# Multiplying exponentials by their inverse sums on ScalarE in place of VectorE, in four attention bodies of an encoder step

## The chip, the cores and the metric

One core of a Trainium2 chip. The time is the device time of one execution in microseconds, the median of a few runs. Before the change it is 1914.42 us (three runs, 1914.21 to 1914.43).

## The reference

One layer of a streaming encoder, run for 256 prompt frames and 32 new frames that share the weights (together 288 columns). In order: half a SwiGLU feed-forward block, a mixer with three groups of attention heads (A: sparse with an indexer, B: sliding window with sinks, C: chunk band), and another half feed-forward block. Cut to what matters here:

```python
def swiglu_ffn(x, g, w_gate, w_up, w_down):
    h = rmsnorm(x, g)
    return (jax.nn.silu(h @ w_gate) * (h @ w_up)) @ w_down

def attend(q, k, v, bias, mask, sinks):
    s = jnp.einsum('btkgd,blkd->bkgtl', qg, k).astype(jnp.float32) * ATTN_SCALE + bias
    p = jax.nn.softmax(s, axis=-1)                  # C
    m = jnp.maximum(jnp.max(s, axis=-1, keepdims=True), sk)      # B, with sinks
    e = jnp.exp(s - m)
    p = e / (jnp.sum(e, axis=-1, keepdims=True) + jnp.exp(sk - m))
    return jnp.einsum('bkgtl,blkd->btkgd', p, v)

x = x + 0.5 * swiglu_ffn(x, *ffn1)
z = rmsnorm(x, g) @ w_in                            # queries, keys, values of all heads
x = x + concat(A, B, C) @ w_out
x = x + 0.5 * swiglu_ffn(x, *ffn2)
```

## The kernel before

Activations lie transposed, 128 features on the partitions and the 288 frames along the row. Every weight matrix is read in strips of 128 output features, 16 tiles of 128x128 at most. Full precision comes from splitting: ScalarE copies the strip `raw` to `w_hi` in a shorter type (line 1117, two halves of 1024 columns), VectorE subtracts to get `w_lo` (line 1444, two halves), and TensorE (PE) does three products for each tile: `w_hi` with the upper and the lower part of the activations (lines 643, 644) and `w_lo` with the upper part (line 645). A strip of 16 tiles is 48 matmuls and takes about 6 us. PE waits for the first half of `w_lo` (`lo_rdy`) before the first tile, for the second before the ninth. SyncE loads strips into two buffers.

The mixer's input projection runs in phases. In phase "cb" (20 strips), the first four strips are projected alone; then come four bodies, each projecting four strips while it does the attention of the pair of heads of groups C and B that the four strips before made. The changed lines count these bodies 0 to 3 and call the attention of the last C and B pair and of group A, which runs in phase "a" and beside "wo", the bodies from 4 on.

A body has five units: 0 and 1 for pair 0 (group C), 2 and 3 for pair 1 (group B), 4 for the 32 new frames of both. Units 0 and 2 hold the later 128 frames, which see 256 keys; units 1 and 3 the earlier 128 frames with 128 keys. A unit holds two heads, so its scores `s_buf` are two rows of 256 or 128 columns for each frame. PE's order in a body is written out (`attention`, line 793): piece 0 (a strip), scores of units 0 to 3, a transpose of values, piece 1, transposes of the probabilities of units 0 and 1 (`tp`, line 749), piece 2, scores of unit 4, outputs of pair 0, transposes of units 2 and 3, piece 3, transposes of unit 4, sums of squares, the other outputs.

ScalarE and VectorE follow in four steps, also in written order (`attention_pairs`, lines 1233 and 1579). In step 0 VectorE adds scale and bias to the scores of units 0 and 1 and takes their maxima (`smax`), and reads a product; ScalarE does their exponentials with sums (`exps`, line 1173); VectorE adds the sink where there is one, takes the inverses of the sums (line 1560) and multiplies the exponentials by them (`inverse`, line 1564); then both split the strip of piece 2. Step 1 does the same for units 2 and 3 and the strip of piece 3, step 2 for unit 4 and piece 0 of the next body, step 3 the key norms and piece 1 of the next body. The engines meet by semaphores alone: `mx_rdy` (maxima), `e_rdy` (exponentials), `r_rdy` (inverses), `p_rdy` (probabilities; PE waits for it in `turn_p`, line 752), `hi_rdy` and `lo_rdy` (splits).

Of the kernel before, what the change touches and what calls it, by code (L numbers as in the profile page):

```python
# [8 lines left out]
ACT = mybir.ActivationFunctionType  # L9
# [104 lines left out]
def encoder_step(nc, x, cak, cav, caki, cbk, cbv, cck, ccv, w_in, w_out, qk_norm, sinks, c_bias, t5_bias,  # L114
# [17 lines left out]
    with ctx:  # L132
        def sb(name, shape, dt=F32, scope=ctx):
            return scope.enter_context(nc.sbuf_tensor(name, shape, dt))

        def sem(name):
            return ctx.enter_context(nc.semaphore(name))
# [87 lines left out]
        s_buf = [sb(f"s_buf{s}", [P, 2, T_P]) for s in range(2)]  # L225
# [13 lines left out]
        einv = [sb(f"einv{s}", [P, 2]) for s in range(2)]  # L239
# [69 lines left out]
        e_rdy = sem("exponentials_ready")  # L309
        r_rdy = sem("inverse_sums_ready")  # L310
        p_rdy = sem("probabilities_ready")
        t_done = sem("probabilities_transposed")
        c_done = sem("transposed_copied")
        pv_done = sem("unit_output_done")
# [43 lines left out]
        NKEY = [T_P, P, PAST + T_S]  # L358
        UNITS = 5
        PAIR_OF, ROWS_OF = (0, 0, 1, 1, None), (0, 1, 0, 1, 2)  # L360
# [8 lines left out]
        def at_once(body):  # L369

            return not (isinstance(body, int) and body >= 4)
# [9 lines left out]
        def v_turn_bank(m):  # L381

            return bank_m if isinstance(m, int) and m == MISC_A0 else bank_t[1]
# [8 lines left out]
        def buf(ph, s):  # L392
            return (ph.n0 + s) % 2
# [103 lines left out]
        RUN0 = 4 * UNITS  # L497
# [26 lines left out]
        def s_slot(U, u):  # L524

            return (U + u) % 4 if isinstance(U, int) and U >= RUN0 else (0, 1, 0, 1, 2)[u]
# [107 lines left out]
        def _(pe):  # L634
# [114 lines left out]
            def turn_p(U, u, slot):  # L749

                b, r = u % 2, ROWS_OF[u]
                pe.wait_ge(p_rdy, U + (u + 1))
                if not (isinstance(U, int) and U + u < 2):
                    pe.wait_ge(c_done, U + (0, 0, 1, 2, 3)[u])
                if r == 2:
                    pe.transpose(bank_t[b][:, 0:P], s_buf[slot][:, 0, 0:P], ident[:, :])
                    mm = pe.transpose(bank_t[b][0:T_S, P:2 * P], s_buf[slot][:, 0, P:P + T_S], ident[:, :])
                else:
                    for c in range(2):
                        for kc in range(NKEY[r] // P):  # L760
                            o = (c * (NKEY[r] // P) + kc) * P
                            mm = pe.transpose(bank_t[b][:, o:o + P], s_buf[slot][:, c, kc * P:(kc + 1) * P], ident[:, :])  # L762
                mm.then_inc(t_done, 1)
# [320 lines left out]
        def _(act):  # L1084
# [61 lines left out]
            def set_deviation(m, b, keys, pairs):  # L1146

                act.wait_ge(m_done, m + 1)

                if keys:  # L1150
                    if not (isinstance(b, int) and b == 0):
                        act.wait_ge(kinv_rdy, b)
                    else:
                        act.wait_ge(rinv_rdy, KEY_NORMS)
                else:
                    act.wait_ge(scale_rdy, scale_no("a", b, pairs[0]) - 1)
                    if isinstance(b, int):
                        act.wait_ge(kinv_rdy, 5)
                c0, c1 = (NT + c for c in scale_cols(pairs))
                act.activation(sd[:, 0 if keys else c0:c1], misc_bank(m)[:, 0 if keys else c0:c1], ACT.Sqrt, bias=eps[:, :]).then_inc(m_free, 1)  # L1160

            def place_v(m, v, cols, bank=None):
                act.wait_ge(m_done, m + 1)
                bank = bank or misc_bank(m)
                act.activation(v[:, 0:2, cols], bank[:, 0:2 * P].rearrange("p (t c) -> p t c", t=2), ACT.Copy)
                act.activation(v[0:T_S, 3, cols], bank[0:T_S, 2 * P:3 * P], ACT.Copy).then_inc(m_free, 1)

            def exps(U, u, sink, sign=1.0):
                b, r = u % 2, ROWS_OF[u]
                n, slot = NKEY[r], s_slot(U, u)  # L1170
                act.wait_ge(mx_rdy, U + (u + 1))
                for c in range(1 if r == 2 else 2):
                    a = act.activation(s_buf[slot][:, c, 0:n], s_buf[slot][:, c, 0:n], ACT.Exp, bias=nmax[b][:, c:c + 1], scale=sign,  # L1173
                                       accum_out=esum[b][:, c:c + 1])
                if sink and r == 2:
                    a = act.activation(esnk[b][HD:P, 0:1], snk[b][HD:P, 0:1], ACT.Exp)
                elif sink:
                    a = act.activation(esnk[b][:, :], snk[b][:, :], ACT.Exp)
                a.then_inc(e_rdy, 1)

            def copy_t(U, u):
                b, r = u % 2, ROWS_OF[u]
                act.wait_ge(t_done, U + (u + 1))
                before = (-1, -1, 2, 2, 0)[u]
                if not (isinstance(U, int) and U + before < 1):

                    act.wait_ge(pv_done, U + before)
                pt = bank_t[b][:, :].rearrange("p (t c) -> p t c", t=4)
                if r == 0:
                    a = act.activation(p_pair[:, :, 1:3, :], pt.rearrange("p (h k) c -> p h k c", h=2), ACT.Copy)  # L1190
                elif r == 1:
                    a = act.activation(p_pair[:, :, 0, :], pt[:, 0:2, :], ACT.Copy)
                else:
                    act.activation(p_t[r][:, 0:1, :], pt[:, 0:1, :], ACT.Copy)
                    a = act.activation(p_t[r][0:T_S, 1:2, :], pt[0:T_S, 1:2, :], ACT.Copy)
                a.then_inc(c_done, 1)

            def out_hi(U, p, tiles):
                act.wait_ge(pv_done, U + (UNITS if p else 2))
                if p == 0:  # L1200
                    a = act.activation(o_hi[:, tiles[0], :, 0:T_P // 2], two_rows(bank_o[:, 0:T_P]), ACT.Copy)
                else:
                    act.activation(o_hi[:, tiles[1], :, :], two_rows(bank_o[:, 0:NT]), ACT.Copy)
                    a = act.activation(o_hi[:, tiles[0], :, T_P // 2:NT // 2], two_rows(bank_o[:, S_OUT[0]]), ACT.Copy)
                a.then_inc(ohi_rdy, 1)
# [27 lines left out]
            def attention_pairs(body, turn, splits, tiles, sums):  # L1233

                U = body * UNITS
                for j in range(4):
                    if j == 0:
                        act.wait_ge(v_out, body * 32 + VOUT_PREP * 32)
                        if not (isinstance(body, int) and body == 0):
                            act.wait_ge(pv_done, U)  # L1240
                        place_v(turn, v_c, slice(0, P), v_turn_bank(turn))
                    elif j < 3:
                        copy_t(U, 2 * j - 2)
                        copy_t(U, 2 * j - 1)
                    else:
                        copy_t(U, 4)
                    if j < 2:
                        exps(U, 2 * j, j == 1)
                        exps(U, 2 * j + 1, j == 1)
                    elif j == 2:  # L1250
                        exps(U, 4, True)
                        out_hi(U, 0, tiles)
                    else:
                        set_deviation(*sums)
                    split(splits[j])
                out_hi(U, 1, tiles)
# [163 lines left out]
        def _(dve):  # L1420
# [130 lines left out]
            def inverse(kind, body, u):  # L1551
                b, r, p = u % 2, ROWS_OF[u], PAIR_OF[u]
                slot = s_slot(body * UNITS, u)
                heads = slice(0, 1 if r == 2 else 2)
                dve.wait_ge(e_rdy, body * UNITS + (u + 1))
                if kind == "cb" and p != 0:
                    rows = slice(HD, P) if r == 2 else slice(0, P)
                    dve.tensor_tensor(esum[b][rows, heads], esum[b][rows, heads], esnk[b][rows, heads], ALU.add).then_inc(sum_sunk, 1)
                    dve.wait_ge(sum_sunk, body * 3 + (r + 1))
                dve.reciprocal(einv[b][:, heads], esum[b][:, heads]).then_inc(r_rdy, 1)  # L1560
                dve.wait_ge(r_rdy, body * UNITS + (u + 1))
                n = NKEY[r]
                for c in range(1 if r == 2 else 2):
                    ins = dve.tensor_scalar(s_buf[slot][:, c, 0:n], s_buf[slot][:, c, 0:n], einv[b][:, c:c + 1], None, ALU.mult)
                ins.then_inc(p_rdy, 1)
# [185 lines left out]
            for ph in phases:  # L1751
# [97 lines left out]
                elif ph.name == "prep":  # L1849
# [12 lines left out]
                    b = buf(ph, 0)  # L1862
# [333 lines left out]
```

## Time and profile before

| | |
|---|---|
| median of three runs | 1914.42 us |
| profiled execution | 1913.98 us |
| its span, first to last instruction | 1912.4 us |
| PE busy | 1905.0 us (100%) |
| VectorE (DVE) busy | 1150.7 us (60%) |
| ScalarE (ACT) busy | 835.6 us (44%) |
| DMA, mean over the span | 178 GB/s |

All times in the rows are microseconds from the start of the span unless marked as ns. A row of a timeline has the start, the length, the engine, the line of the kernel, the operation, what it writes and reads, and how many follow each other; in brackets the idle time before it and what ended that. A row's length is that of the whole run of instructions from the first start to the last end; instructions on one engine overlap a little, so the next may start before the end of the one before. PEld is the loading of weights into PE, which runs beside its matmuls. Shares of the whole span say little here: feed-forward and attention have different limits, so the four bodies (868 to 992 us) are looked at apart.

### The profile page before, as it was taken

To read this page: it belongs to the slowest core of one execution; us is meant where nothing else is said; L and a number is where in the kernel's file an instruction comes from. 1 tells how busy PE (TensorE), PEld (TensorE's weight loads), DVE (VectorE), ACT (ScalarE), POOL (GpSimd) and SP (SyncE) were. 2 spreads that over 40 slices of the span, in tenths; PEclk is the share of its full clock that TensorE was granted. 3 is DMA by queue.
4 is the path that set the end of the run, shared out by engine and by line. 5 is a ranking of instruction groups with operands and counts; after the bars stand their busy time and mean duration, and the time that the engine had idled before them with its cause. 6 is when DMAs were issued, how large, how long until landed. Compare 5 with 4: busy or idle time off the path is not lost.

```text
span 1912.4 us, 41753 instructions
## 1 busy us (share of the span) xinstructions
PE 1905.0 (100%) x15725; PEld 1885.5 (99%) x15725; DVE 1150.7 (60%) x1714; ACT 835.6 (44%) x1223; POOL 131.1 (7%) x237
## 2 busy tenths in 40 slices
PE   9999999999999999999999999999999999999999
PEld 8999999999999999999998999999999999999999
DVE  7555445555555566588888765555545555455554
ACT  6443333343333344445668644333334443333332
POOL 1000000000000000124665000000000000000000
DMA  7555555555555555655554555555555555555564
GB/s 270 180 180 172 185 171 178 179 183 176 184 176 175 175 176 176 194 167 167 164 183 123 165 180 177 182 177 174 181 174 181 179 178 175 184 175 178 180 196 154
DMA packets 102298, 340.62 MB, mean 178 GB/s; under 512 B 12661, under 2 KB 17317, under 8 KB 102224
## 3 DMA queue, kind: packets, MB, share of 16 engines
q1 hardware_dynamic: 95856, 329.41, 52.9%
q0 software_dynamic: 3984, 8.11, 1.7%
q10 hardware_dynamic: 2400, 2.33, 0.3%
q8 instruction: 36, 0.59, 0.1%
q14 instruction: 22, 0.18, 0.0%
HBM read 335.10 MB, written 5.28 MB: 178 GB/s over the span
## 4 chain that ended last, share of the span: by engine, by line
PE 97%; DVE 1%; ACT 1%; issue 0%; DMA 0%; POOL 0%; SPq 0%; POOLq 0%; DVEq 0%; ACTq 0%
PE bank L643 32%; PE bank L645 31%; PE bank L644 31%; PE bank L745 1%; PE bank L762 0%; PE bank L777 0%; DMA raw<-in_w_ffn_gate 0%; PE bank L711 0%; PE bank L963 0%; PE bank L789 0%; DVE h_hi_and_lo L1713 0%; ACT s_buf L1173 0%; PE bank L780 0%; DVE w_lo L1444 0%; DVE w_lo L1721 0%
## 5 line engine op out<-in xcount | busy, mean ns | idle before, releaser
L643 PE MATMUL bank<-h_hi_and_lo,w_hi 128*128 128x288 f32 x3344 | 961.2, 287 | 1.8 <-DVE w_lo L1721 1.6
L644 PE MATMUL bank<-h_hi_and_lo,w_hi 128*128 128x288 f32 x3344 | 956.5, 286 | 0.0
L645 PE MATMUL bank<-h_hi_and_lo,w_lo 128*128 128x288 f32 x3344 | 956.4, 286 | 0.0
L1444 DVE TENSOR_TENSOR w_lo<-raw,w_hi 128x1024 fp32r<-128x1024 f32 x634 | 727.9, 1189 | 205.4 <-ACT w_hi L1117 205.1
L1117 ACT ACTIVATE w_hi<-raw 128x1024 fp32r<-128x1024 f32 x634 | 616.7, 1020 | 289.5 <-PE bank L645 272.6
L643 PEld LDWEIGHTS bank<-h_hi_and_lo,w_hi 128*128 128x128 f32 x3344 | 632.0, 189 | 6.8 <-issue 3.0
L644 PEld LDWEIGHTS bank<-h_hi_and_lo,w_hi 128*128 128x128 f32 x3344 | 632.2, 189 | 0.2
L645 PEld LDWEIGHTS bank<-h_hi_and_lo,w_lo 128*128 128x128 f32 x3344 | 632.1, 189 | 0.0
L643 PE MATMUL bank<-gu_hi_and_lo,w_hi 128*128 128x288 f32 x1376 | 393.5, 286 | 0.0
L644 PE MATMUL bank<-gu_hi_and_lo,w_hi 128*128 128x288 f32 x1376 | 393.5, 286 | 0.0
L645 PE MATMUL bank<-gu_hi_and_lo,w_lo 128*128 128x288 f32 x1376 | 393.5, 286 | 0.0
L643 PEld LDWEIGHTS bank<-gu_hi_and_lo,w_hi 128*128 128x128 f32 x1376 | 260.1, 189 | 0.0
L644 PEld LDWEIGHTS bank<-gu_hi_and_lo,w_hi 128*128 128x128 f32 x1376 | 260.1, 189 | 0.0
L645 PEld LDWEIGHTS bank<-gu_hi_and_lo,w_lo 128*128 128x128 f32 x1376 | 260.1, 189 | 0.0
L1350 ACT ACTIVATE gu_hi_and_lo<-gu 128x288 f32 (+1 forms) x86 | 40.6, 472 | 348.8 <-DVE gu L1790 348.8
L1346 ACT ACTIVATE g_sig<-g_act 128x288 f32<-128x288 f32 x86 | 38.1, 442 | 240.6 <-DVE g_act L1468 240.6
L1832 DVE SCALAR_TENSOR_TENSOR gains_and_x<-bank,gains_and_x 128x288 f32 (+1 forms) x96 | 43.9, 457 | 155.7 <-PE bank L645 154.8
L1468 DVE TENSOR_TENSOR u_act<-bank,rstd 128x288 f32<-128x288 f32 x86 | 39.3, 457 | 122.6 <-PE bank L645 122.6
L1468 DVE TENSOR_TENSOR g_act<-bank,rstd 128x288 f32<-128x288 f32 x86 | 39.3, 458 | 76.4 <-PE bank L645 76.3
L1795 DVE TENSOR_TENSOR gu_hi_and_lo<-gu,gu_hi_and_lo 128x288 f32 (+1 forms) x86 | 39.5, 459 | 70.0 <-ACT gu_hi_and_lo L1350 69.9
L643 PE MATMUL bank<-o_hi_and_lo,w_hi 128*128 128x288 f32 x256 | 73.9, 289 | 0.0
L644 PE MATMUL bank<-o_hi_and_lo,w_hi 128*128 128x288 f32 x256 | 73.2, 286 | 0.0
(227 smaller groups left out, 964.6 us busy)
## 6 DMA issues: line engine op xcount, KB each, us to landing
raw<-in_w_ffn_gate SPq DMA_DIRECT2D x168, 512.0 KB, 4.5
raw<-in_w_ffn_up SPq DMA_DIRECT2D x168, 512.0 KB, 4.6
raw<-in_w_ffn_down SPq DMA_DIRECT2D x96, 512.0 KB, 3.8
raw<-in_w_in SPq DMA_DIRECT2D x74, 512.0 KB, 4.7
raw<-in_w_ffn_down SPq DMA_DIRECT2D x64, 384.0 KB, 4.2
raw<-in_w_out SPq DMA_DIRECT2D x32, 512.0 KB, 4.5
raw<-in_w_ffn_down SPq DMA_DIRECT2D x32, 448.0 KB, 4.3
bias_rev<-bias_vectors POOLq DMA_DIRECT2D x11, 256.0 KB, 5.9
```

The source lines that it names most:

```text
L643: pe.matmul(out, w_hi[b][:, k, :], hi, start=(k == first_k), stop=False)
L644: pe.matmul(out, w_hi[b][:, k, :], lo, start=False, stop=False)
L645: mm = pe.matmul(out, w_lo[b][:, k, :], hi, start=False, stop=(k == last_k))
L745: mm = pe.matmul(score_place(body, u, c), q[p][half, FULL[r]], kt[p][half, KEY0[r]:KEY0[r] + NKEY[r]], start=True, stop=True)
L1117: act.activation(w_hi[b][:, k, :], raw_tile(ph, j, s)[:, k, :], ACT.Copy).then_inc(hi_rdy, 1)
L1346: act.activation(g_sig[:, :], g_act[:, :], ACT.Silu).then_inc(sig_rdy, 1)
L1350: act.activation(gu_hi[:, j, :, :], two_rows(gu[:, :]), ACT.Copy).then_inc(guh_rdy, 1)
L1444: dve.tensor_tensor(w_lo[b][:, k, :], raw_tile(ph, j, s)[:, k, :], w_hi[b][:, k, :].bitcast(F32), ALU.subtract)\
L1468: return dve.tensor_tensor(dst, (early_bank(n) or bank_w[b])[rows, cols], rstd[rows, cols], ALU.mult)
L1795: dve.tensor_tensor(gu_lo[:, j, :, :], two_rows(gu[:, :]), gu_hi[:, j, :, :].bitcast(F32), ALU.subtract).then_inc(gul_rdy, 1)
L1832: dve.scalar_tensor_tensor(dst, src[:, 0:NT], factor, xT[:, d, :], ALU.mult, ALU.add)\
```

## The change

In bodies 0 to 3 the multiplies of units 0 and 2 (256 keys, two heads each) are taken out of VectorE's `inverse`, which returns behind the inverse. ScalarE gets a function `weigh`: it waits for the inverse and does the two multiplies as `Copy` with the inverse as scale of each partition. It is called in steps 0 and 1 behind both units' exponentials and ahead of the split. A new semaphore `p_act` tells PE that units 0 and 2 are done; the counts of `p_rdy` are renumbered. Units 1, 3 and 4 and all bodies from 4 on stay as they were.

```diff
@@ turn_p (PE)
-                pe.wait_ge(p_rdy, U + (u + 1))
+                if U < RUN0 and r == 0:
+                    pe.wait_ge(p_act, U // UNITS * 2 + (PAIR_OF[u] + 1))
+                elif U < RUN0:
+                    pe.wait_ge(p_rdy, U // UNITS * 3 + (u // 2 + 1))
+                else:
+                    pe.wait_ge(p_rdy, RUN0 // UNITS * 3 + U - RUN0 + (u + 1))
@@ ScalarE
+            def weigh(U, u):
+
+                b, slot = u % 2, s_slot(U, u)
+                act.wait_ge(r_rdy, U + (u + 1))
+                for c in range(2):
+                    a = act.activation(s_buf[slot][:, c, 0:NKEY[0]], s_buf[slot][:, c, 0:NKEY[0]], ACT.Copy, scale=einv[b][:, c:c + 1])
+                a.then_inc(p_act, 1)
...
                     if j < 2:
                         exps(U, 2 * j, j == 1)
                         exps(U, 2 * j + 1, j == 1)
+                        weigh(U, 2 * j)
@@ inverse (VectorE)
                 n = NKEY[r]
+                if r == 0 and at_once(body):
+                    return
```

ScalarE before, steps 0 and 1 of body 0 (`p_pair` holds transposed probabilities, `esnk` the exponentials of the sinks):

```order
L1173 ACTIVATE s_buf,esum<-s_buf,nmax 128x256 x2
L1173 ACTIVATE s_buf,esum<-s_buf,nmax 128x128 x2
L1117 ACTIVATE w_hi<-raw 128x1024 x2
L1190 ACTIVATE p_pair<-bank 128x2x256
L1192 ACTIVATE p_pair<-bank 128x2x128
L1173 ACTIVATE s_buf,esum<-s_buf,nmax 128x256 x2
L1178 ACTIVATE esnk<-snk 128x2
L1173 ACTIVATE s_buf,esum<-s_buf,nmax 128x128 x2
L1178 ACTIVATE esnk<-snk 128x2
L1117 ACTIVATE w_hi<-raw 128x1024 x2
```

The same place of the changed kernel (its line numbers are a little higher):

```order
L1179 ACTIVATE s_buf,esum<-s_buf,nmax 128x256 x2
L1179 ACTIVATE s_buf,esum<-s_buf,nmax 128x128 x2
L1192 ACTIVATE s_buf<-s_buf,einv 128x256 x2
L1123 ACTIVATE w_hi<-raw 128x1024 x2
L1204 ACTIVATE p_pair<-bank 128x2x256
L1206 ACTIVATE p_pair<-bank 128x2x128
L1179 ACTIVATE s_buf,esum<-s_buf,nmax 128x256 x2
L1184 ACTIVATE esnk<-snk 128x2
L1179 ACTIVATE s_buf,esum<-s_buf,nmax 128x128 x2
L1184 ACTIVATE esnk<-snk 128x2
L1192 ACTIVATE s_buf<-s_buf,einv 128x256 x2
L1123 ACTIVATE w_hi<-raw 128x1024 x2
```

Two pairs of activations are new, each directly ahead of a split (`w_hi`); nothing else moved on this engine.

VectorE before, the end of step 1 of body 0 (`esum` the sums, `einv` their inverses, `z_q` a product that is read):

```order
L1468 TENSOR_TENSOR z_q<-bank,rstd 128x288
L1558 TENSOR_TENSOR esum<-esum,esnk 128x2
L1560 RECIPROCAL einv<-esum 128x2
L1564 TENSOR_SCALAR s_buf<-s_buf,einv 128x256 x2
L1558 TENSOR_TENSOR esum<-esum,esnk 128x2
L1560 RECIPROCAL einv<-esum 128x2
L1564 TENSOR_SCALAR s_buf<-s_buf,einv 128x128 x2
L1444 TENSOR_TENSOR w_lo<-raw,w_hi 128x1024 x2
```

And in the changed kernel:

```order
L1483 TENSOR_TENSOR z_q<-bank,rstd 128x288
L1573 TENSOR_TENSOR esum<-esum,esnk 128x2
L1575 RECIPROCAL einv<-esum 128x2
L1573 TENSOR_TENSOR esum<-esum,esnk 128x2
L1575 RECIPROCAL einv<-esum 128x2
L1581 TENSOR_SCALAR s_buf<-s_buf,einv 128x128 x2
L1459 TENSOR_TENSOR w_lo<-raw,w_hi 128x1024 x2
```

The two multiplies of 256 columns are gone, and the rest keeps its order.

## Rows read from the trace of the kernel before

**Rows 1.** The page: span, and the engines' shares of the last chain.

```profile
span 1912.4 us, 41753 instructions
...
PE 97%; DVE 1%; ACT 1%; issue 0%; DMA 0%; POOL 0%; SPq 0%; POOLq 0%; DVEq 0%; ACTq 0%
```

**Rows 2.** Stretches, bodies 0, 3: length, busy PE, PEld, DVE, ACT, POOL, clock, DMA.

```profile
868.40:899.00 30.60, 30.60 (x284) 29.40 (x284) 26.29 (x61) 18.91 (x42) 14.18 (x21) 1.00 0.54 168
...
960.40:991.60 31.20, 30.97 (x284) 29.41 (x284) 27.84 (x66) 18.96 (x44) 18.05 (x31) 1.00 0.54 167
```

**Rows 3.** PE's waits in the four bodies: us in total, times, longest.

```profile
PE bank L643 <- DVE w_lo L1444: 0.2, 1, 0.2
```

**Rows 4.** Timeline of PE: transposes, then the next piece's first matmul (bodies 0, 3).

```profile
882.17 0.82 PE L762 MATMUL bank<-ident,s_buf 128*128 128x128 f32 x6
882.75 0.37 PE L643 MATMUL bank<-h_hi_and_lo,w_hi 128*128 128x288 f32 x1
...
889.88 0.87 PE L762 MATMUL bank<-ident,s_buf 128*128 128x128 f32 x6
890.57 0.36 PE L643 MATMUL bank<-h_hi_and_lo,w_hi 128*128 128x288 f32 x1
...
974.16 0.82 PE L762 MATMUL bank<-ident,s_buf 128*128 128x128 f32 x6
975.21 0.36 PE L643 MATMUL bank<-h_hi_and_lo,w_hi 128*128 128x288 f32 x1 [0.23 <-DVE w_lo L1444]
```

**Rows 5.** Timeline of ACT: the splits for pieces 2 and 3.

```profile
880.07 0.19 ACT L1173 ACTIVATION_READ_ACCUMULATOR s_buf<-s_buf,nmax 128x1 f32 x1
880.17 1.99 ACT L1117 ACTIVATE w_hi<-raw 128x1024 fp32r<-128x1024 f32 x2
...
887.79 1.99 ACT L1117 ACTIVATE w_hi<-raw 128x1024 fp32r<-128x1024 f32 x2
...
941.25 1.99 ACT L1117 ACTIVATE w_hi<-raw 128x1024 fp32r<-128x1024 f32 x2
...
972.46 1.99 ACT L1117 ACTIVATE w_hi<-raw 128x1024 fp32r<-128x1024 f32 x2
```

**Rows 6.** Timeline of DVE: low parts for pieces 2 and 3, and around them.

```profile
881.24 2.36 DVE L1444 TENSOR_TENSOR w_lo<-raw,w_hi 128x1024 fp32r<-128x1024 f32 x2
883.52 0.87 DVE L1526 SCALAR_TENSOR_TENSOR s_buf<-bank,q_scale,bias_rev 128x256 f32<-128x256 f32 x2
...
887.35 0.17 DVE L1560 RECIPROCAL einv<-esum 128x2 f32<-128x2 f32 x1
887.55 0.91 DVE L1564 TENSOR_SCALAR s_buf<-s_buf,einv 128x256 f32<-128x256 f32 x2
...
889.21 1.22 DVE L1444 TENSOR_TENSOR w_lo<-raw,w_hi 128x1024 fp32r<-128x1024 f32 x1
...
942.62 2.35 DVE L1444 TENSOR_TENSOR w_lo<-raw,w_hi 128x1024 fp32r<-128x1024 f32 x2
...
973.53 1.53 DVE L1444 TENSOR_TENSOR w_lo<-raw,w_hi 128x1024 fp32r<-128x1024 f32 x1 [0.24 <-ACT w_hi L1117]
...
976.12 0.86 DVE L1526 SCALAR_TENSOR_TENSOR s_buf<-bank,q_scale,bias_rev 128x256 f32<-128x256 f32 x2
```

**Rows 7.** Groups in the four bodies: count | busy us, mean ns | idle before.

```profile
L1564 DVE TENSOR_SCALAR s_buf<-s_buf,einv 128x256 f32<-128x256 f32 x16 | 6.3, 437 | 0.3
```

**Rows 8.** ACT, timeline rows and groups: what is nearest to the added copies.

```profile
878.40 0.51 ACT L1173 ACTIVATE s_buf<-s_buf,nmax 128x256 f32<-128x256 f32 x1
878.81 0.19 ACT L1173 ACTIVATION_READ_ACCUMULATOR s_buf<-s_buf,nmax 128x1 f32 x1
...
10.90 1.45 ACT L1127 ACTIVATE h_hi_and_lo<-gains_and_x 128x288 fp32r<-128x288 f32 x3
...
L1127 ACT ACTIVATE h_hi_and_lo<-gains_and_x 128x288 fp32r<-128x288 f32 x26 | 13.6, 552 | 1.7 <-DMA gains_and_x<-in_gains_and_x 1.7
...
L1299 ACT ACTIVATE w_hi<-raw 128x256 fp32r<-128x256 f32 x2 | 0.8, 410 | 0.1
```

More of the change, by code:

```diff
@@ L311, in encoder_step @@
         p_rdy = sem("probabilities_ready")
+        p_act = sem("probabilities_ready_by_scalar")
         t_done = sem("probabilities_transposed")
```

## The prediction

> **What bounds the kernel now.** I read the page's busy times and chain first. The chain that ended last is 97% PE over a span of 1912.4 us [rows 1], so a VectorE or ScalarE instruction costs time only where PE is made to wait. The second view is the table of stretches, one per attention body: the first of the four bodies that the diff touches lasts 30.6 us and the last 31.2, with PE busy for all of it but 0.2 us in the last, and the granted clock at 1.00 (its upper level) [rows 2]. VectorE is busy 26 to 28 us of each, ScalarE 19 us: neither is full, both have places where they are late.
>
> The list of PE's waits names one such wait, for a low half of a weight strip (`w_lo`), 0.2 us [rows 3]. The timeline shows more than that list. Between pieces of projection PE does six 128x128 transposes and then the first matmul of the next piece. Where nothing is late this matmul starts 0.58 us after the transposes (882.17 to 882.75); ahead of piece 3 of body 0 it takes 0.69 (889.88 to 890.57), and ahead of piece 2 of body 3 1.05 (974.16 to 975.21) [rows 4]. The VectorE row that makes the first half of that strip's `w_lo` started at 889.21 and took 1.22; 889.21 + 1.36 = 890.57 [rows 4, 6]. The same 1.36 or 1.37 us from start of `w_lo` to start of the piece holds at five places of these bodies: piece 3 of all four and piece 2 of body 2. So there PE already starts when the first half of the strip's low part is there; on the three other pieces 2 the slack is 0.15 and 0.21 us (bodies 0 and 1) and none (body 3, where the half took 1.53 us instead of 1.22 [rows 6]). All these small stalls together (start distances above 0.58) come to about 1.2 us. Whatever delays the first half of `w_lo` in front of pieces 2 and 3 delays PE, nearly one for one.
>
> **What the change does to that chain.** In front of pieces 2 and 3 each engine goes through the same order: ScalarE does the exponentials and then the two halves of `w_hi`; VectorE does sums, inverses, multiplies and then the two halves of `w_lo`, each of which waits for its half of `w_hi`. Where VectorE waits, `w_lo` starts 1.07 us after `w_hi` (972.46 to 973.53) [rows 5, 6]; I take 1.08.
>
> Removed from VectorE: two multiplies of 256 columns at each of two places in four bodies, 16 in all, 437 ns each by the mean, 6.3 us busy [rows 7]. The pair in front of piece 3 of body 0 takes 0.91 us [rows 6].
>
> Added to ScalarE: the same 16 as copies with a per-partition scale, placed before the two `w_hi` halves, so `w_hi` moves back by the pitch of two. No such row exists at 256 columns. The nearest: the exponential of 256 columns with a per-partition bias lasts 0.51, and the next instruction starts 0.41 us after it [rows 8]. A copy with a per-partition scale at 288 columns lasts 0.552, three take 1.45, a pitch of (1.45 - 0.55)/2 = 0.45 us; it also reads and writes with a stride [rows 8]. A plain copy of 256 columns lasts 0.410; less the overlap of 0.10 seen at the exponential, 0.31 [rows 8]. So between 0.31 and 0.45; I take 0.40, nearest to the row with the same number of columns and a pointer operand. A pair is A = 0.80 us, with ends 0.62 and 0.90. No table load is added: `w_hi`, a copy too, follows the exponentials with no load between them (880.07, 880.17) [rows 5].
>
> The added wait: the copies wait for VectorE's inverse. In front of piece 3 of body 0 that ends at 887.35 + 0.17 = 887.52, and ScalarE is free for it at 887.79 [rows 5, 6]; 0.27 us to spare. In front of piece 2 there is as much or more. Behind the waiting copy stand `w_hi` and, behind that, the copies of the transposes; PE wants the probabilities (transposes at 882.17 and 889.88) a microsecond after the copies end, so the new semaphore itself costs nothing.
>
> Step by step, with the margin = start of `w_lo` now, minus start of `w_hi`, minus 1.08 (what VectorE was late by itself):
> - Piece 2, body 0: 881.24 - 880.17 - 1.08 = about 0, so `w_lo` starts 0.81 later. Body 1 repeats it within 0.01 us: 0.80.
> - Piece 2, body 2: 942.62 - 941.25 - 1.08 = 0.29, so 0.51 later.
> - Piece 2, body 3: starts 0.81 later, but the first half then takes 1.22 and not 1.53. Two halves pass in 2.28 us (881.24 to 883.52), so VectorE is free at 972.46 + 0.80 + 1.08 + 2.28 = 976.62 in place of 976.12: 0.50 later [rows 5, 6].
> - From there VectorE's next units, the exponentials and the split for piece 3 all start later by the same amount, since ScalarE waits there for VectorE's maxima. PE's delay at piece 2 is so carried into the next term and isn't counted twice.
> - Piece 3: margin 889.21 - 887.79 - 1.08 = 0.34 [rows 5, 6], and 0.34 or 0.35 in all four bodies. It adds A - 0.34 = 0.46 to each.
>
> Delay of PE at piece 3: body 0 0.81 + 0.46 = 1.27; body 1 1.26; body 2 0.51 + 0.45 = 0.96; body 3 0.50 + 0.46 = 0.96. Sum 4.45 us; in A it is 8A - 1.95. Behind piece 3 nothing is given back: the later splits of a body and the next body's first steps follow PE's own products, and have two microseconds and more to spare. The loads wait for `w_lo` of the strip before, so they move with it. In the other phases no line changes.
>
> The profiled execution took 1913.98, the runs' median is 1914.42, 0.44 more; both get 4.45: 1918.43 and **1918.87**. I forecast 1918.9 us. What can be told from no change is 0.2%, or 3.83 us; my sum is above it by 0.6, and falls below it if a pair costs less than 0.72 us. By the ends of A the sum is 3.0 and 5.25.
>
> The Trainium skill speaks of this choice. "Perfetto Trace Analysis", section "Optimizing Scalar/DVE Operations", puts ScalarE's overhead on SBUF at about 93 ns of engine time. By an estimate from that page (93 ns and 256 columns at 1.2 GHz) a copy would take 0.31 us, the pair 0.61, and the sum would be 2.9 us. The exponential's row, with its 0.41, speaks against it, so I hold that the pointer operand is paid too.
>
> **Rivals.**
> - Cheap copies: a pitch of 0.31 to 0.35 as in the plain copy [rows 8]. Sum 3.0 to 3.7, 1917.4 to 1918.1 us: slower, but not by 0.2%. Against it: the pitch of both rows with a pointer. Chance 0.16.
> - Not slower: the multiplies leave VectorE, the busier of the two, and its lateness at piece 3 (0.34) and at piece 2 of body 2 (0.29) is what holds PE up there. If ScalarE took the copies in time that it waits (it stands idle for VectorE's maxima and PE's transposes), only the gain would stay: at most the stalls of 1.2 us, 1913.2, and 1914.4 if nothing waits either way. It decides in favour where a pair delays `w_hi` by less than 1.95/8 = 0.24 us. Against it: in the order the copies stand directly before the split, behind exponentials that end late. The skill's same section says that work may go to ScalarE where DVE is saturated, which would bring this out; the stretches (26 to 28 of 31 us busy) show it near that but not there. Chance 0.10.
> - Dear copies: the pitch of 0.45, or a wait for the inverse that ends late by over 0.27 us because VectorE shares its time with POOL there. Sum 5.3 to 6.5, 1919.7 to 1920.9. Against it: the spare 0.27. Chance 0.14.
>
> **How the numbers follow.** My forecast (3.7 to 5.2, 1918.1 to 1919.6) has 0.60. Slower by over 0.2%: 0.55 of that and 0.14 of dear copies, 0.69. Within 0.2%: the rest of mine (0.05), cheap copies (0.16), and most of not slower (0.07), 0.28. Faster by over 0.2% would need 3.8 us where PE stalls 1.2 in all: 0.03. The range 1917.0 to 1920.3 takes in both ends of A and leaves out not slower and the far end of dear copies.
>
> **What the changed profile would show.** Copies of 0.49 us with a pitch of 0.40 before `w_hi`, 16 of them, and 6.3 us less on VectorE; VectorE now waiting for `w_hi` at all eight places, some 1.2 to 1.7 us each (what it loses there plus the multiplies that it no longer does); PE waiting for `w_lo` ahead of pieces 2 and 3 in every body; bodies about 1.0 to 1.3 us longer, the first 31.9 and the last 32.2 us; nothing else longer. It would be wrong if the copies stand in ScalarE's idle time, if a body after its piece 3 gets time back, or if PE waits for the transposed probabilities and not for `w_lo`.

## The result and the profile after

The changed kernel takes 1918.52 us (median of 11 runs, 1917.84 to 1919.48), the kernel before 1913.79 (11 runs, 1912.79 to 1914.71): a ratio of 1.0026, 95% interval 1.0019 to 1.0034, or 4.7 us slower. The profiled execution took 1919.29 us over a span of 1917.7, 5.3 more than before [rows 1]. One execution in the experiments, of the kernel with a bias load held back, took 2474.20 us, where its ten others took 1917.67 to 1918.99.

The added copies first: a summary of their line, and ScalarE's timeline in front of pieces 2 and 3 of body 0 (start, length, engine, line).

```profile
L1192 ACT ACTIVATE s_buf<-s_buf,einv x16: 492/494/497, 880.3 to 984.6; 128x256 f32<-128x256 f32 x16
```

```profile
880.35 0.89 ACT L1192 ACTIVATE s_buf<-s_buf,einv 128x256 f32<-128x256 f32 x2
881.15 1.99 ACT L1123 ACTIVATE w_hi<-raw 128x1024 fp32r<-128x1024 f32 x2
...
888.77 0.89 ACT L1192 ACTIVATE s_buf<-s_buf,einv 128x256 f32<-128x256 f32 x2
889.57 1.99 ACT L1123 ACTIVATE w_hi<-raw 128x1024 fp32r<-128x1024 f32 x2
```

Sixteen copies of 494 ns, and `w_hi` follows a pair 0.80 us after its start: a pitch of 0.40. In [rows 5] `w_hi` started at 880.17 and 887.79.

VectorE's timeline at the same places, then what VectorE and what PE waited for in the four bodies (total us, times, longest):

```profile
882.22 2.36 DVE L1459 TENSOR_TENSOR w_lo<-raw,w_hi 128x1024 fp32r<-128x1024 f32 x2 [0.88 <-ACT w_hi L1123]
...
890.64 2.36 DVE L1459 TENSOR_TENSOR w_lo<-raw,w_hi 128x1024 fp32r<-128x1024 f32 x2 [0.80 <-ACT w_hi L1123]
```

```profile
DVE w_lo L1459 <- ACT w_hi L1123: 6.5, 8, 0.9
```

```profile
PE bank L644 <- DVE w_lo L1459: 3.3, 8, 0.4
```

The rows of the 256-key multiplies [rows 7] are gone: 6.3 us less work on VectorE, and 6.5 us of waiting for `w_hi` there, where before only one wait stood, of 0.24 [rows 6]. VectorE now waits for as long as it was relieved. PE, which waited once for `w_lo` [rows 3], waits at all eight places.

PE's timeline shows it at body 0:

```profile
882.36 0.82 PE L768 MATMUL bank<-ident,s_buf 128*128 128x128 f32 x6
883.59 0.36 PE L644 MATMUL bank<-h_hi_and_lo,w_hi 128*128 128x288 f32 x1 [0.42 <-DVE w_lo L1459]
...
890.71 0.88 PE L768 MATMUL bank<-ident,s_buf 128*128 128x128 f32 x6
892.01 0.36 PE L644 MATMUL bank<-h_hi_and_lo,w_hi 128*128 128x288 f32 x1 [0.42 <-DVE w_lo L1459]
```

From the transposes to the next piece 1.23 and 1.30 us, in [rows 4] 0.58 and 0.69. And 882.22 + 1.37 = 883.59, 890.64 + 1.37 = 892.01: the piece still starts 1.37 us after its `w_lo`.

The first matmul of each piece can be followed like this through all kernels. The table says how much later it comes than in the first execution of before, with the lateness that the execution already had at the start of body 0 subtracted (those starts scatter from -0.59 to +1.10 us between executions, where the code is the same in all). Columns: pieces 2 and 3 of bodies 0 to 3; the third and fourth piece after body 3 (pieces there are thirds of a pair of strips); a late piece, at 1069. "1st", "2nd" and "3rd" are profiled executions of the same kernel; the later ones belong to the experiments below. All later tables are of this kind.

| | b0 p2 | b0 p3 | b1 p2 | b1 p3 | b2 p2 | b2 p3 | b3 p2 | b3 p3 | 1002.6 | 1009.5 | 1069 |
|---|---|---|---|---|---|---|---|---|---|---|---|
| predicted | 0.81 | 1.27 | 2.07 | 2.53 | 3.04 | 3.49 | 3.99 | 4.45 | 4.45 | 4.45 | 4.45 |
| changed, 1st profile | 0.66 | 1.26 | 1.86 | 2.51 | 3.01 | 3.47 | 3.68 | 4.14 | 4.51 | 5.19 | 5.16 |
| changed, 2nd | 0.67 | 1.28 | 1.90 | 2.57 | 3.08 | 3.55 | 3.76 | 4.23 | 4.55 | 5.24 | 5.24 |
| changed, 3rd | 0.66 | 1.26 | 1.86 | 2.52 | 3.02 | 3.48 | 3.68 | 4.15 | 4.71 | 5.38 | 5.33 |
| before, 2nd | -0.01 | 0.00 | -0.01 | 0.00 | -0.10 | -0.29 | -0.31 | -0.31 | -0.32 | -0.31 | -0.35 |

Two things come out. The bodies cost 4.14 to 4.23 us, stepwise nearly as forecast. Then, behind piece 3 of body 3, where no line was changed, PE loses another 1.0 to 1.2 us. From the last column on nothing is added: in the first profile PE is 5.34 us later at 1069 (5.16 and the 0.18 of the start of body 0), and the span is 5.3 longer.

### The profile page after: what moved, and what is told of

Read it like the earlier page. It is cut to its first block, busy times and chain, and to the rows that moved or that the text cites. A ratio compares the mean times of both kernels' runs of the same rounds, so it can differ in the third digit from the quotient of the medians.

```text
span 1917.7 us, 41761 instructions
## 1 busy us (share of the span) xinstructions
PE 1906.1 (99%) x15725; PEld 1885.3 (98%) x15725; DVE 1143.9 (60%) x1698; ACT 842.0 (44%) x1239; POOL 122.4 (6%) x237
## 4 chain that ended last, share of the span: by engine, by line
PE 94%; DVE 2%; ACT 2%; issue 1%; DMA 0%; POOL 0%; SPq 0%; POOLq 0%; DVEq 0%; ACTq 0%
PE bank L644 31%; PE bank L646 31%; PE bank L645 31%; DVE w_lo L1459 1%; ACT s_buf L1179 0%; PE bank L746 0%; DVE s_buf L1541 0%; ACT w_hi L1123 0%; DMA raw<-in_w_ffn_gate 0%; DVE nmax L1553 0%; PE bank L768 0%; PE bank L969 0%; ACT s_buf L1192 0%; PE bank L712 0%; PE bank L783 0%
```

## The experiments

The theory: ScalarE's copies stand in the chain exponentials, `w_hi`, `w_lo`, PE, and each pair delays it by 0.80 us; VectorE's relief is worth nothing. The rivals: the loss belongs to one of the two steps; it comes from the new semaphore or the renumbered counts; VectorE's relief gives something back that hides a larger cost. A second question is the loss behind body 3.

### One step at a time

The copies of unit 0 only, or of unit 2 only; the other stays with VectorE. The edits of this section are shown against the changed kernel, shortened, with `...` for what is left out.

```diff
-                        weigh(U, 2 * j)
+                        if j == 0:        # second kernel: j == 1
+                            weigh(U, 2 * j)
...
-                if r == 0 and at_once(body):
+                if u == 0 and at_once(body):        # second kernel: u == 2
```

> The copies of step 0 alone (units 0) on ScalarE; units 2 are multiplied on VectorE as before. Theory (a pair of copies ahead of the split delays the low half of the strip by what it lasts, 0.80 us, less what VectorE was late by itself): 0.8, 0.8, 0.5 and 0.2 to 0.5 us in bodies 0 to 3, 2.3 to 2.6 in all, about 1916.2 us, and in front of piece 3 nothing is added to it. Rival (PE waits for probabilities from ScalarE): no wait for w_lo ahead of piece 3 but one ahead of the transposes. Rival (the relief of VectorE counts): half of the changed kernel's loss or less.

> The copies of step 1 alone (units 2) on ScalarE; units 0 are multiplied on VectorE as before. Theory: nothing ahead of piece 2, 0.46 us ahead of piece 3 in each body, 1.84 in all; with step 0 alone the two add up to the changed kernel's 4.1 to 4.5 in the bodies. Behind body 3 the changed kernel lost about 1 us more, where ScalarE waited 1.5 us for a strip's load; if that comes from VectorE standing idle ahead of piece 3 it shows here too: 1915.6 us without, 1916.7 with it.

Step 0 alone: 1916.38 us (ratio 1.0015, 1.0006 to 1.0024). Step 1 alone: 1916.50 (1.0015, 1.0006 to 1.0024); the kernel before, beside them, 1913.67.

| | b0 p2 | b0 p3 | b1 p2 | b1 p3 | b2 p2 | b2 p3 | b3 p2 | b3 p3 | 1002.6 | 1009.5 | 1069 |
|---|---|---|---|---|---|---|---|---|---|---|---|
| step 0 | 0.65 | 0.79 | 1.39 | 1.59 | 2.09 | 2.10 | 2.30 | 2.30 | 2.29 | 2.30 | 2.32 |
| step 1 | 0.00 | 0.47 | 0.46 | 0.93 | 0.82 | 1.08 | 0.63 | 1.71 | 2.42 | 3.10 | 3.10 |

Step 0 delays pieces 2, step 1 pieces 3, and the parts come near the whole: 2.30 + 1.71 = 4.01 against 4.14 to 4.23 for both. The loss is two terms of one kind, not one bad place. That the sum comes so near is in part luck: step 1's 1.71 isn't four times 0.46. Its pieces 3 pay 0.47, 0.47, 0.26 and 1.08, and PE gets back 0.11 and 0.45 ahead of pieces 2 of bodies 2 and 3. In body 2 the 0.11 and the 0.20 that is missing from 0.46 are the two stalls that the second profile of before lacks too; what gives the 0.45 isn't shown. For the 1.08 of body 3 VectorE's and GpSimd's timelines show the place.

```profile
973.92 1.90 POOL L2045 TENSOR_TENSOR o_hi_and_lo<-z_prep,o_hi_and_lo 128x288 fp32r<-128x288 f32 x1 [0.18 <-POOL o_hi_and_lo L2042]
```

```profile
973.94 2.96 DVE L1460 TENSOR_TENSOR w_lo<-raw,w_hi 128x1024 fp32r<-128x1024 f32 x2
```

The two run side by side, and both are long: `w_lo` 2.96 where it is 2.36 elsewhere, GpSimd's 1.90 where it is 0.90 to 0.96. The 0.60 goes through the next unit's exponentials to piece 3: 0.46 + 0.60 = 1.06.

### Work for both, work for neither

First VectorE keeps its multiplies and ScalarE does copies of the same shape at the same places, into a buffer that nobody reads. Then nobody multiplies: that kernel leaves out the division by the sums for these units.

```diff
+                    act.activation(spare[:, c, :], kc_cache[:, 2 * c:2 * c + 2, :].rearrange("p k n -> p (k n)"), ACT.Copy, scale=mean_any[:, 0:1])
...
-                if r == 0 and at_once(body):
-                    return
```

```diff
-                    pe.wait_ge(p_act, U // UNITS * 2 + (PAIR_OF[u] + 1))
+                    pe.wait_ge(r_rdy, U + (u + 1))
...
-                        weigh(U, 2 * j)
```

> VectorE keeps all its multiplies as before the change, and ScalarE makes the same two pairs of copies in the same places, waiting for the same inverses, from a constant tile into a spare one. Theory: the four bodies are as long as in the changed kernel, 4.1 to 4.5 us over before, since the copies ahead of the split are late by themselves and what VectorE is spared is worth nothing: 1917.9 us, or 1918.5 with the wait behind body 3. Rival (the relief of VectorE is worth its 0.34 us a place): 2 to 3 us slower than the changed kernel, 1921 us.

> The multiplies of units 0 and 2 of bodies 0 to 3 are left out on both engines (so the result there lacks the division by the sums); PE waits for the inverses in their place. What is left is the relief of VectorE alone. Theory: PE can only win its small stalls, 1.0 to 1.2 us in all, 1912.7 us. Rival (VectorE is the bound of these bodies): the 6.3 us that it is spared show in good part, 1909 to 1911 us.

Both: 1919.07 us (1.0028, 1.0017 to 1.0038). Neither: 1913.44 (0.9999, 0.9990 to 1.0008).

| | b0 p2 | b0 p3 | b1 p2 | b1 p3 | b2 p2 | b2 p3 | b3 p2 | b3 p3 | 1002.6 | 1009.5 | 1069 |
|---|---|---|---|---|---|---|---|---|---|---|---|
| both | 0.68 | 1.28 | 1.89 | 2.54 | 3.04 | 3.50 | 3.71 | 4.17 | 4.53 | 5.21 | 5.20 |
| neither | 0.00 | -0.07 | -0.05 | -0.05 | -0.15 | -0.35 | -0.31 | -0.52 | -0.52 | -0.51 | -0.53 |

With both, the row is that of the changed kernel within 0.05 us, though VectorE does all its old work and PE waits for the old semaphore: neither the relief nor the new semaphore matters. With neither, what the removal is worth shows alone: 0.5 us in the trace against the first execution of before, 0.2 against the second, nothing that the times can tell; the 1.0 to 1.2 us expected for it were not there. PE's waits for `w_lo` in the two (the four bodies):

```profile
PE bank L644 <- DVE w_lo L1454: 3.3, 8, 0.4
```

```profile
PE bank L643 <- DVE w_lo L1449: 0.3, 1, 0.3
```

That also answers whether a better place is near: even with no multiplies of these units at all there is nothing measurable to win, so no other place for them can win it.

### Twice the copies

The changed kernel with a second pair behind each pair, which writes a buffer that nobody reads.

```diff
+                for c in range(2):
+                    act.activation(spare[:, c, :], kc_cache[:, 2 * c:2 * c + 2, :].rearrange("p k n -> p (k n)"), ACT.Copy, scale=mean_any[:, 0:1])
...
                         weigh(U, 2 * j)
+                        idle_copies(U, 2 * j)
```

> The changed kernel with another pair of copies behind each pair, from a constant tile into a spare one (16 more, 1.60 us at each of the eight places). Theory: the loss in the bodies is 8A - 1.95 with A = 1.60, 10.85, less 0.3 for a late start in body 3 that was in the execution before: 10.5 to 10.9, 1924.5 us, or 1925.5 with the wait behind body 3. Rival (the copies stand in time that ScalarE has to spare, and the loss comes from the new semaphore or the loads): 1918.5 to 1920 us.

Measured 1924.63 us (1.0059, 1.0045 to 1.0074); the kernel before, beside it, 1913.42. In the bodies PE loses 10.56 us, and the sum in A at A = 1.60 gives 8 x 1.60 - 1.95 = 10.85. From one pair to two the loss grows by 10.56 - 4.14 = 6.4 us, eight times 0.80: nothing absorbs any part. ScalarE's timeline and PE's waits in that kernel:

```profile
880.21 0.90 ACT L1193 ACTIVATE s_buf<-s_buf,einv 128x256 f32<-128x256 f32 x2
881.01 0.89 ACT L1200 ACTIVATE spare<-kc_cache,mean_any 128x256 f32<-128x256 f32 x2
881.80 1.99 ACT L1124 ACTIVATE w_hi<-raw 128x1024 fp32r<-128x1024 f32 x2
```

```profile
PE bank L645 <- DVE w_lo L1469: 9.7, 8, 1.2
```

The waits go from 3.3 to 9.7, again by 6.4.

### The copies between the halves of w_hi

```diff
-                        weigh(U, 2 * j)
...
-                    split(splits[j])
+                    if j < 2:
+                        split(splits[j], (0,))
+                        weigh(U, 2 * j)
+                        split(splits[j], (1,))
+                    else:
+                        split(splits[j])
```

> The changed kernel with each pair of copies between the two halves of the split in place of ahead of it. Theory: the first half of w_lo is no longer late from the copies; its second half is, by some 0.6 us at the end, which is VectorE's start into step 1: 0.3 us in bodies 0 and 1, nothing or a small gain in bodies 2 and 3, so 0.2 to 0.6 us over before, 1914.2 us, or 1915.2 if the wait behind body 3 stays. Rival (PE waits for the probabilities, which now come 1 us later): ahead of the transposes up to 0.3 us a place and no gain against the changed kernel.

Measured 1917.87 us (1.0022, 1.0014 to 1.0031): a miss for the theory's number, and the rival's sign came instead. In the bodies PE does lose less, 1.69 us in place of 4.14, and no longer at `w_lo`. PE's waits in the four bodies:

```profile
PE bank L768 <- ACT s_buf L1192: 1.8, 5, 0.4
```

The probabilities are now what comes last: the first half of `w_hi` gains, and the copies behind it lose part of that again. And then this kernel loses 2.27 us behind body 3, the most of all.

### The loss behind body 3

What GpSimd, SyncE and ScalarE do there, first in the changed kernel, then in the second profile of before (timelines).

```profile
985.73 0.48 POOL L2012 TENSOR_SCALAR q_n<-z_q,qk_cols 128x256 f32<-128x256 f32 x1 [0.31 <-PE bank L740]
987.15 0.77 POOL L1980 DMA_DIRECT2D bias_rev<-bias_vectors  x1 [0.95 <-POOL q_n L2012]
...
988.65 0.85 SPq L578 DMA_DIRECT2D raw<-in_w_in  x2
...
997.62 2.00 ACT L1123 ACTIVATE w_hi<-raw 128x1024 fp32r<-128x1024 f32 x2 [1.50 <-DMA raw<-in_w_in]
...
1000.51 2.44 DVE L1459 TENSOR_TENSOR w_lo<-raw,w_hi 128x1024 fp32r<-128x1024 f32 x2
...
1004.50 0.51 ACT L1179 ACTIVATE s_buf<-s_buf,nmax 128x256 f32<-128x256 f32 x1 [1.06 <-DVE nmax L1553]
```

```profile
981.02 2.55 POOL L1995 TENSOR_SCALAR q_n<-z_q,qk_cols 128x256 f32<-128x256 f32 x1 [0.31 <-PE bank L739]
983.48 0.85 SPq L577 DMA_DIRECT2D raw<-in_w_in  x2
984.51 0.77 POOL L1963 DMA_DIRECT2D bias_rev<-bias_vectors  x1 [0.94 <-DVE z_prep L1526]
...
990.83 1.99 ACT L1117 ACTIVATE w_hi<-raw 128x1024 fp32r<-128x1024 f32 x2
```

In the kernel before, GpSimd multiplies the queries for 2.55 us, and its bias load (256 KB) goes out 1.03 us after SyncE's load of a strip; ScalarE needn't wait for the strip, 7.35 us later. In the changed kernel the same multiply takes 0.48 us and the bias load goes out 1.50 us ahead of the strip's. ScalarE waits 1.50 us for the strip, `w_lo` comes late on VectorE, which has it ahead of the next scores, and the exponentials of the next body wait for their maxima. PE then starts the third and the fourth piece behind body 3 late.

The theory: the order of the two loads decides. To test it, the changed kernel holds the second pair's bias load, in all four bodies, until the scores of unit 4 have their bias. At this place that is some 2.4 us later, behind the strip's load.

```diff
-                    pool.wait_ge(s_add, body * UNITS + (2 * p - 3))
+                    pool.wait_ge(s_add, body * UNITS + (0 if p == 1 and project == "cb" else 2 * p - 3))
...
-                    load_bias(nxt[1], at, 1, b)
+                    load_bias(nxt[1], at, 1, b, "cb")
```

> The changed kernel, with POOL's load of the second pair's bias table held until the scores of unit 4 have their bias, so that it is issued behind the load of the strip for piece 1 of the next body. Theory: the bodies stay 4.1 us over before, and the wait of 1.5 us for that strip behind body 3 goes, with the 1.05 us that followed it: 1917.5 us. Rival (that wait has another cause, or is one execution's chance): the wait stays, or the time is that of the changed kernel, 1918.5.

To see whether the loss is chance, further profiles were taken: two of the changed kernel, one of this one, one of the kernel before.

> The changed kernel once more, for a second profile. The question is the 1.05 us that the first profile shows behind body 3, where the strip for piece 1 of the next body landed late. If the order of the two loads decides it (the bias load issued about 1.2 us before the strip's load, because GpSimd's multiply of q_n took 0.48 us there), then the multiply takes 0.5 us again, w_hi of that strip starts more than 8 us after its load is issued, and PE loses about 1.0 us between body 3 and the second step behind it; time 1918.9 to 1919.5. If it is chance in the transfers, the loss is absent in some profiles with the same order of the loads.

> As the run before it, a third profile of the changed kernel. Order of the loads decides: the loss of about 1.0 us is there whenever the bias load goes out first. Chance: it is there in some and not in others, with the times of those without it near 1918.2.

> The kernel with the bias load of that place held back, once more. If the order of the loads decides, PE loses nothing behind body 3 again, and the time is about 1917.7 to 1918.2. If it is chance, the loss can be there with the load held back.

> The kernel before, a second profile. If the order of the loads decides, GpSimd's multiply there takes about 2.5 us beside VectorE's low part, the bias load goes out after the strip's load, and the strip is there in time (w_hi starts within 7.4 us of the load's issue); 1913.4 to 1914.4. If it is chance, the late strip may show here too. It also tells whether ScalarE's late start of 0.3 us in body 3 of the first profile comes again: if not, PE reaches the end of body 3 about 0.3 us earlier, counted from the start of body 0.

Every profile taken, by the timelines: the time from the issue of the bias load to that of the strip's (negative: strip first), from the bias load to `w_hi`, ScalarE's wait for the strip, and what PE loses from piece 3 of body 3 to the piece at 1009.5.

| | bias to strip | bias to w_hi | wait | PE loses |
|---|---|---|---|---|
| before, 1st and 2nd | -1.02, -1.03 | 6.33, 6.32 | none | 0.00 |
| step 0 | -1.03 | 6.32 | none | 0.00 |
| neither | -1.03 | 6.46 | none | 0.01 |
| bias later, 1st and 2nd | -0.91 | 6.45, 6.44 | none | 0.03 |
| between the halves | 0.63 | 10.37 | 2.81 | 2.27 |
| both | 1.49 | 10.44 | 1.49 | 1.04 |
| changed, 1st, 2nd, 3rd | 1.50 | 10.47, 10.41, 10.66 | 1.50, 1.45, 1.70 | 1.05, 1.01, 1.23 |
| step 1 | 1.51 | 10.82 | 1.85 | 1.39 |
| twice the copies | 2.31 | 9.88 | none | 0.00 |

In all six profiles with the strip's load first here, nothing is lost. Where the bias load goes first by 0.6 to 1.5 us, the strip is there 10.4 to 10.8 us after the bias load's issue, whenever it was itself issued, and PE loses 1.0 to 2.3 us. With 2.3 us of lead the strip is in time again. Turning the order in one kernel (bias later) takes the loss away in both its profiles, and all three of the changed kernel have it: in the traces it is no chance, and without this order it isn't there.

The order alone is not enough, though. In bodies 0 to 2 of the changed kernel (first profile) the bias load goes out ahead of the strip's too, by 1.72, 1.51 and 1.51 us. The place in body 2 (timelines):

```profile
955.26 0.77 POOL L1980 DMA_DIRECT2D bias_rev<-bias_vectors  x1 [0.94 <-POOL q_n L2012]
...
956.77 0.85 SPq L578 DMA_DIRECT2D raw<-in_w_in  x2
...
964.68 2.00 ACT L1123 ACTIVATE w_hi<-raw 128x1024 fp32r<-128x1024 f32 x2 [0.46 <-DMA raw<-in_w_in]
```

ScalarE waits 0.71 us, not at all and 0.46 there; `w_hi` starts 8.18, 7.35 and 7.91 us after the strip's load is issued, and not 8.97 as behind body 3, and PE loses nothing by it: with the order turned (bias later) the four bodies cost 4.25 and 4.23 us, with it as it was 4.14 to 4.23. Why the same order costs more behind body 3 stays open.

The times confirm it only in part. The profiled executions with the bias load held back took 1917.67 and 1918.05 us, those of the changed kernel 1919.29, 1918.70 and 1919.67, the second of before 1913.08. But the kernel with the load held back has a median of 1918.45 over its eleven timed runs (1.0026, 1.0016 to 1.0035), where some 1917.5 was to be expected, and 1918.52 is that of the changed kernel. The two intervals are over 2.8 us wide and cannot part the two; whether executions that weren't profiled have the loss each time stays open.

## Why the prediction was right or wrong

**The cost of a pair.** Right: the pair takes 0.80 us and delays `w_hi` by it. That decides both rivals of size: cheap copies (a pitch of 0.31 to 0.35) and dear copies (0.45, or a late inverse) fell with the pitch of 0.40; no copy waited for the inverse. The estimate from the Trainium skill ("Perfetto Trace Analysis", section "Optimizing Scalar/DVE Operations"), 0.31 us a copy, fell too: here it is 0.40, as the exponential's row had it.

**The path.** Right: the loss enters through the first half of `w_lo` at pieces 2 and 3, with 1.37 us from its start to the piece. Step by step it fits where it was worked out from margins: 0.51 and 0.45 at pieces 2 and 3 of body 2 (measured 0.50 and 0.46), 0.46 at piece 3 of body 3 (0.46). At pieces 2 of bodies 0 and 1 PE loses 0.66 and 0.60 instead of 0.81 and 0.80, because of the slack of 0.15 and 0.21 named there; the next piece 3 takes the rest (0.60, 0.65), and the bodies come out at 1.26 and 1.25 as forecast. The lengths of the first and last body are 31.86 and 31.89 us, forecast 31.9 and 32.2.

**Piece 2 of body 3.** Mis-sized: 0.50 forecast, 0.21 measured. The step took the place of ScalarE's exponentials from the trace of before. The rows of PE and ScalarE ahead of them, in the second profile of before and in the changed kernel:

```profile
967.33 0.27 PE L726 MATMUL bank<-ident,z_v 128*128 128x128 f32 x1
968.01 0.38 ACT L1165 ACTIVATE v_c<-bank 128x256 f32<-128x256 f32 x1 [5.99 <-PE bank L726]
```

```profile
971.82 0.27 PE L727 MATMUL bank<-ident,z_v 128*128 128x128 f32 x1
972.21 0.38 ACT L1171 ACTIVATE v_c<-bank 128x256 f32<-128x256 f32 x1 [5.14 <-PE bank L727]
```

ScalarE takes the transposed values 0.41 us after PE's last transpose before (968.01 - 967.60), and 0.12 after it in the changed kernel (972.21 - 972.09). What held it back before, in both profiles, no view names; these 0.29 us are the difference. Against the second profile of before, which lacks two stalls of 0.1 and 0.2 in body 2, the four bodies cost 4.14 + 0.31 = 4.45 us. That the sum is then exactly the forecast is two small errors that cancel. The forecast time, 1918.87, came near the measured 1918.52 in the same way: the median of three runs that it starts from was 0.63 above that of eleven, and the change that it adds was 0.28 too small.

**"Behind piece 3 nothing is given back ... In the other phases no line changes."** The first half held, the second did not follow from it. This is the step that failed: unchanged code behind the bodies lost 1.0 to 1.2 us in the traces, where an engine off the path (GpSimd) issued a load earlier than SyncE. "The loads wait for `w_lo` of the strip before, so they move with it" holds for the strip's load alone; the bias load hangs on GpSimd's multiply. With this term the traces give 5.2 to 5.3 us against the first profile of before and 5.5 to 5.7 against the second, the medians 4.7, the forecast 4.45.

**Not slower, or VectorE's relief.** Refuted: with VectorE's work kept, the loss is the same; with the work gone and no copies, nothing measurable is won. The stalls of 1.2 us, named as the most that could be won, were mostly not VectorE's multiplies: 0.2 to 0.5 of them went.

**VectorE's waits for `w_hi`.** At all eight places, but 0.8 to 0.9 us each and not 1.2 to 1.7. VectorE spends part of the freed time waiting for the sums of the exponentials instead, ahead of its inverse. The first line is the changed kernel, the second the kernel before (waits of VectorE in the four bodies):

```profile
DVE einv L1575 <- ACT s_buf L1179: 5.7, 7, 1.1
```

```profile
DVE einv L1560 <- ACT s_buf L1173: 3.2, 4, 1.1
```

Nothing in the sum hung on it.

## What to carry to other kernels

Which engine is less busy doesn't decide where work should go; what matters is whose instruction the busy engine waits for last, and what the moved work stands ahead of. ScalarE was idle for over a third of each body, but the copies stood directly ahead of the split that PE comes to wait for, and 6.4 us of copies (eight pairs of 0.80) became 4.1 to 4.5 us of loss, though VectorE was relieved of 6.3. Where the added work can't stand behind the thing that others wait for, price it in full at each place, less the margin of the engine that follows. And when one engine becomes idle at some place, look at what its neighbours' loads do there: an unchanged phase can lose time where two transfers change their order.

## What the runs showed of the hardware that was not expected

GpSimd's multiply of 128x256 elements lasts as little as 0.48 us and as much as 2.55, and the long ones looked at stand beside VectorE's `w_lo`. Two summaries of it (minimum, median and maximum in ns), of the kernel before and of the changed one:

```profile
L1995 POOL TENSOR_SCALAR q_n<-z_q,qk_cols x16: 478/1706/2547, 858.4 to 1051.7; 128x256 f32<-128x256 f32 x16
```

```profile
L2012 POOL TENSOR_SCALAR q_n<-z_q,qk_cols x16: 474/477/2493, 858.6 to 1057.1; 128x256 f32<-128x256 f32 x16
```

The long one at 981.88 in the first execution of before runs beside the `w_lo` at 981.80 that takes 2.36 us; the short one at 985.73 in the changed kernel falls into VectorE's wait of 0.80 us ahead of 986.12. The other direction shows in the 2.96 us of `w_lo` beside GpSimd's 1.90 (step 1 alone). The Trainium skill ("Perfetto Trace Analysis", section "Optimizing Scalar/DVE Operations") states that GpSimd and VectorE share a read port of SBUF. These runs agree with that as the cause, with a factor of five on GpSimd and 0.6 us on VectorE, but none of them tests it apart.

Behind body 3, a load of 256 KB from GpSimd's queue went with a late strip (two loads of 512 KB from SyncE's queue) when it was issued 0.6 to 1.5 us ahead: `w_hi` of that strip started 7.35 to 7.5 us after its load's issue where the strip went first, with no wait, and 8.9 to 9.7 where the bias load did (997.62 - 988.65 = 8.97 in the changed kernel). It is no rule for every place: in bodies 0 to 2 of the changed kernel the same order gave 7.35 to 8.18, and with neither engine multiplying a strip of body 0 was waited for 0.91 us though its load went first; PE lost nothing by either.
